# Attention loop of a hybrid decoder layer: all score banks of a job computed in one step instead of two

## The chip, the cores and the metric

The kernel runs on one core of a Trainium2 chip. The metric is the device time of one execution in microseconds (us), as the median of several runs. Less is better.

## What is computed

One post-norm decoder layer over 512 tokens of width 1024, in fp32, with three sublayers: a hybrid mixer, a cross attention over 256 memory rows, and a SwiGLU. The change lies in the mixer, which has three attention branches side by side:

```python
proj = x @ w_in + b_in                        # q, k, v of A, B, C, forget gates, merge gates
# A: 4 heads x 3 dilation groups, banded, T5 bias; groups combined by softmax denominators
# B: 8 query heads over 2 kv heads, window 128, T5 bias, learned sinks
# C: 4 heads, causal, logit bias from cumulated log forget gates
s = einsum(q, k) + bias;  s = where(mask, s, -1e30)
m = max(s);  p = exp(s - m);  o = einsum(p / sum(p), v)
merged = g0*(o_a @ w_a) + g1*(o_b @ w_b) + g2*(o_c @ w_c)
x = layer_norm(ALPHA*x + merged @ w_out)
```

## The kernel before, in words

Every engine has its program written out by hand, and the engines meet only at semaphores. The large matrix products are split into two fp32r parts and run as three matmuls each (`mm3`, L1588); they fill TensorE for most of the time. Between the input projection and the gate stage lies the attention loop, the part that the change touches.

**Jobs.** The attention work is cut into 12 jobs (`make_jobs`, L167). Jobs 0 to 3 are the heads of A, jobs 4 to 7 pairs of heads of B, jobs 8 to 11 heads of C. A job's scores fill up to four PSUM banks; job j's bank b always lies in PSUM bank b (`score_bank`, L511), so banks 0 to 3 are used by one job after the other. Jobs 4 to 8 and job 10 have four banks, jobs 9 and 11 have two. The scores of jobs 0 to 3 are computed ahead of the loop, in the stretch `FRONT`.

**Steps.** The loop has 22 steps (`N_GROUP_PAIRS`), each for a pair of transposition groups. In step i TensorE (L1858 to L1868)
- transposes the probabilities of groups 2i+2 and 2i+3 into PSUM banks 4 and 5 (`turn_probs`, L1741, matmul at L1753). It first waits until the copies of groups 2i and 2i+1 are out of these banks (`pt_act`, `pt_dve`);
- computes scores (`scores`, L1705, matmuls at L1718, for C also L1725), if `SIDE[i]` lists any. `side_work` (L233) lists banks 0 and 1 of a job in one step and banks 2 and 3 in the next: job 4 in steps 1 and 2, job 5 in 3 and 4, job 6 in 5 and 6, job 7 in 7 and 8, job 8 in 10 and 11, job 9 in 12, job 10 in 14 and 15, job 11 in 16;
- in some steps transposes a row of reciprocals (`turn_recip`, L1756, L1762);
- multiplies the transposed probabilities of groups 2i and 2i+1 by V (`times_v`, L1765, matmul at L1789).

VectorE in step i (L1343 to L1356) copies group 2i+3 out of PSUM (`pt_drain`, L1209), now and then inverts the sums of a job (L1193, L1194), drains an output accumulator (`out_drain`, L1229, L1234), and then drains the banks of `SIDE[i]` (`scores_out`, L1157): for each unit of a bank it adds the bias and takes the extreme value (L1181), which is one custom instruction and one that reads the accumulator; the second raises `neg_ready`. ScalarE in step i (L924 to L934) copies group 2i+2 out of PSUM (L865), copies parts of accumulators (L871, L877) and applies the exponential to the banks of the step before, `SIDE[i - 1]` (`exps`, L838, L851).

**What orders a bank's reuse.** `scores` takes the banks of its job two at a time. Ahead of each two it waits on `neg_ready` until VectorE has drained what an earlier job left in these banks:

```python
for some in [banks[i:i + 2] for i in range(0, len(banks), 2)]:
    for b in some:
        prev = [(jj, bb) for jj, bb in bank_list if jj < j and score_bank(jj, bb) == score_bank(j, b)]
        if prev:
            pe.wait_ge(neg_ready, bank_units_end[prev[-1]])
```

`neg_ready` is one counter, raised in VectorE's order of drains.

Names in short, as used below: T is `turn_probs`, V is `times_v`, S01 and S23 are the scores of banks 0 and 1 and of banks 2 and 3, "4;3" is bank 3 of job 4.

Of the kernel before, what the change touches and what calls it, by code (L numbers as in the profile page):

```python
# [44 lines left out]
N_AH, N_G = 4, 3  # L45
# [96 lines left out]
N_SELF = 12  # L142
# [90 lines left out]
def side_work(jobs):  # L233

    side = [[] for _ in range(N_GROUP_PAIRS)]
    for j in range(4, N_SELF):
        first = 2 * j - 7 if j < 8 else C_SCORES_AT[j - 8]
        for b in range(len(jobs[j][0])):  # L240
            side[first + b // 2].append((j, b))
    return side


def build_layer(nc, A, out):
    JOBS = make_jobs() + make_cross_jobs()
    SIDE = side_work(JOBS)
# [62 lines left out]
    with ExitStack() as ctx:  # L310
# [193 lines left out]
        def exps_of(j):  # L504

            return units_before[(j | 1) + 1 if JOBS[j][1][0][2] == "C" else j + 1]

        RECIP_AT = [n + 1 for n in out_begin[N_AH:]]
        SUMS_AT = {j: 2 * j - 4 if j < 8 else C_SCORES_AT[j - 7] + 1 for j in [4, 5, 6, 7, 8, 10]}

        def score_bank(j, b):  # L511
            return b
# [305 lines left out]
        def _(act):  # L818
            def split(p):

                c = chunk_of(p)
                if p == 0:
                    act.wait_ge(first_in, 16)
                else:
                    act.wait_ge(raw_in[c % 2], arrive_at[c])
                if p >= 2:
                    act.wait_ge(piece_done, slot_spent(p))
                src, hi, _ = raw_piece(p)
                act.copy(hi, src).then_inc(hi_done, 1)  # L829
# [43 lines left out]
            def recip_copy(k):  # L873

                act.wait_ge(recip_ps, k - N_AH + 1)
                act.wait_ge(acc_dve, k - 1)
                act.copy(qk[:, T_RECIP + k % 2, :], ps[:, acc_bank(2 * k + 2), :]).then_inc(recip_out, 1)  # L877
# [46 lines left out]
            for i in range(N_GROUP_PAIRS):  # L924
# [4 lines left out]
                if i == 0:  # L929
                    split(PG + 1)  # L930
                if i in RECIP_AT:
                    recip_copy(N_AH + RECIP_AT.index(i))
                for j, b in SIDE[i - 1] if i else []:
# [653 lines left out]
        def _(pe):  # L1587
# [94 lines left out]
            def operands(kind, h, t):  # L1682

                rows = slice(t * P, (t + 1) * P)
                band = slice(max(t - 1, 0) * P, (t + 1) * P)
                half_ = slice(64 * (h % 2), 64 * (h % 2) + 64)
                if kind == "X":
                    return qx[half_, h // 2, rows], kx[half_, h // 2, :]
                if kind == "A0":
                    return qk[half_, T_QA + h // 2, rows], qk[half_, T_KA + h // 2, band]  # L1690
                if kind in ("A1", "A2"):
                    g = int(kind[1])
                    return qk[half_, T_QA + 2 * g + h // 2, rows], qk[half_, T_KA + 2 * g + h // 2, rows]
                if kind == "B":
                    return qk[half_, T_QB + h // 2, rows], qk[half_, T_KB + h // 4, band]
                return qk[half_, T_QC + h // 2, rows], qk[half_, T_KC + h // 2, 0:(t + 1) * P]

            def key_gates(h, n):

                half_ = slice(64 * (h % 2), 64 * (h % 2) + 64)
                return pick[half_, h % 2, h // 2:h // 2 + 1].to_broadcast([64, P]), gates_t[half_, 0:n]

            def scores(j, banks=None):  # L1705

                banks = list(banks or range(len(JOBS[j][0])))
# [5 lines that stand above are left out]
                    n_units = len(JOBS[j][0][some[0]])  # L1713
                    for u in range(n_units):
                        for b in some:
                            kind, h, t, c0, cols, at = JOBS[j][0][b][u]
                            q, k = operands(kind, h, t)
                            ins = pe.matmul(ps[:, score_bank(j, b), c0:c0 + cols], q, k, start=True, stop=kind != "C")  # L1718
                            if u == n_units - 1 and kind != "C":
                                ins.then_inc(score_ps, 1)  # L1720
                        for b in some:
                            kind, h, t, c0, cols, at = JOBS[j][0][b][u]
                            if kind == "C":
                                one, gates = key_gates(h, cols)
                                ins = pe.matmul(ps[:, score_bank(j, b), c0:c0 + cols], one, gates, start=False, stop=True)  # L1725
                                if u == n_units - 1:
                                    ins.then_inc(score_ps, 1)
# [13 lines left out]
            def turn_probs(n):  # L1741

                j, g = group_list[n]
                offs = JOBS[j][1][g][0]
                if N_AH <= j < N_SELF:
                    pe.wait_ge(exp_done, exps_of(j))
                else:
                    pe.wait_ge(prob_pool if j in POOL_SCALES else prob_dve, scaled_for(j, g))
                if n >= 2:
                    pe.wait_ge(*pt_count(n - 2))  # L1750
                kind = JOBS[j][1][g][2]
                for c, at in enumerate(offs):
                    ins = pe.transpose(ps[:, 4 + n % 2, c * P:(c + 1) * P], prob_at(kind, at, P), ident[:, :])  # L1753
                ins.then_inc(pt_ps, 1)

            def turn_recip(k):  # L1756

                pe.wait_ge(recip_wide, k - N_AH + 1)
                pe.wait_ge(acc_dve, k)
                for t in range(TT):  # L1760
                    cols = slice(t * P, (t + 1) * P)
                    ins = pe.transpose(ps[:, acc_bank(2 * k + 2), cols], qk[:, T_WIDE + k % 2, cols], ident[:, :])  # L1762
                ins.then_inc(recip_ps, 1)

            def times_v(n):  # L1765

                work = []
                for i in (n, n + 1):
                    j, g = group_list[i]
                    _, products, kind, h, first, last = JOBS[j][1][g]  # L1770
                    m = acc_of[i]
                    pe.wait_ge(*pt_count(i))
                    if first and m >= FIRST_X + 2:
                        pe.wait_ge(oxl_done, m - 2 - FIRST_X + 1)
                    elif first and 4 <= m < FIRST_X:
                        pe.wait_ge(acc_dve, m // 2 - 1)
                        if m // 2 > N_AH:
                            pe.wait_ge(recip_out, m // 2 - N_AH)
                    src = ptx if j >= N_SELF else pt
                    work.append([(ps[acc_half(kind, h), acc_bank(m), q0:q0 + cols], v_tile(kind, h, kb),  # L1780
                                  src[:, i % PT_SLOTS, c0:c0 + cols], first and x == 0, last and x == len(products) - 1)
                                 for x, (kb, c0, cols, q0) in enumerate(products)])
                a, b = work
                for x in range(max(len(a), len(b))):
                    for one in (a, b):
                        y = x - max(len(a), len(b)) + len(one)
                        if y >= 0:
                            dst, lhs, rhs, start, stop = one[y]
                            ins = pe.matmul(dst, lhs, rhs, start=start, stop=stop, skip_group_check=True)  # L1789
                            if y == len(one) - 1:  # L1790
                                ins.then_inc(av_done, 1)
# [66 lines left out]
            for i in range(N_GROUP_PAIRS):  # L1858
                if i + 1 < N_GROUP_PAIRS:
                    turn_probs(2 * i + 2)  # L1860
                    turn_probs(2 * i + 3)
                if SIDE[i]:
                    scores(SIDE[i][0][0], [b for _, b in SIDE[i]])
                if i in RECIP_AT:
                    turn_recip(N_AH + RECIP_AT.index(i))
                if i == 0:
                    pe.wait_ge(proj_out, 22 + 9)
                times_v(2 * i)  # L1868
# [215 lines left out]
```

## Time and profile before

| what | value |
|---|---|
| median of 3 runs | 907.95 us (907.76, 907.95, 908.62) |
| the profiled execution's own time | 909.56 us |
| its span (first to last instruction) | 907.8 us, granted clock 0.997 |
| attention loop in the trace | 197.6 to 257.75 us |
| steps 1 to 8 (scores of jobs 4 to 7) | 201.15 to 224.84 us |

The times of the rows are in us from the start of the span. In the timeline a row begins with its start and its duration; matmuls overlap, so the length of a phase of TensorE is the distance from its start to the start of the phase behind it. "xN" counts instructions; one fp32 matmul of the program stands as several. In brackets is how long the engine sat idle before the row, and what released it.

### The profile page before, as it was taken

The numbers are of one execution on the slowest core, as the hardware profiler recorded it, in microseconds if no ns is written. First come the engines' busy times: TensorE is split into PE (matmuls) and PEld (weight loads), VectorE is DVE, ScalarE is ACT, GpSimd is POOL, SyncE is SP. The second block draws the span as 40 slices with busy tenths as digits, with TensorE's granted clock in tenths as the row PEclk, the third lists the DMA queues.
The fourth block names the chain that finished last, engine by engine and source line by source line (L and its number), as shares of the span: only waits on it lengthen the run. The fifth ranks groups of instructions, "written<-read, shape, count | busy, mean of one in ns | idle before, by whom it ended". The sixth has DMA issues, their size and how long they took to land.

```text
span 907.8 us, 11620 instructions
## 1 busy us (share of the span) xinstructions
PE 882.0 (97%) x4547; PEld 732.8 (81%) x4547; DVE 424.1 (47%) x795; ACT 290.8 (32%) x536; POOL 59.0 (7%) x87
## 2 busy tenths in 40 slices
PE   7999999999999999999999889999999999999996
PEld 7988887777678888888889679888888888888885
DVE  4244347669632525353766784333333333422344
ACT  3112157129642232222424742222222222111221
POOL 2100000080310000000020020000000000000001
PEclk9999999999999999999999999999999999999999
DMA  7524630321002333326515101233322224222321
GB/s 267 158 93 106 151 94 24 113 80 42 2 1 94 106 105 107 98 92 231 191 42 170 57 6 50 93 103 110 106 94 92 92 92 139 93 93 97 109 96 69
DMA packets 70022, 89.88 MB, mean 99 GB/s; under 512 B 2701, under 2 KB 61911, under 8 KB 69983
## 3 DMA queue, kind: packets, MB, share of 16 engines
q1 hardware_dynamic: 69599, 88.92, 30.3%
q0 software_dynamic: 384, 0.43, 0.3%
q8 instruction: 26, 0.43, 0.2%
q14 instruction: 13, 0.11, 0.0%
HBM read 86.81 MB, written 2.52 MB: 98 GB/s over the span
## 4 chain that ended last, share of the span: by engine, by line
PE 91%; ACT 3%; DVE 3%; issue 1%; DMA 1%; POOL 1%; SPq 0%; DVEq 0%; POOLq 0%; ACTq 0%
PE ps L1590 27%; PE ps L1592 27%; PE ps L1591 27%; PE ps L1789 3%; PE ps L1753 2%; PE ps L1718 2%; ACT prob L851 2%; PE ps L1627 1%; DVE w_lo L1083 1%; PE ps L2061 1%; DMA x_nat<-in_x 1%; PE ps L2062 1%; PE ps L2063 1%; ACT w_hi L829 0%; DVE resid L1423 0%
## 5 line engine op out<-in xcount | busy, mean ns | idle before, releaser
L1590 PE MATMUL ps<-xt_hi,w_hi 128*128 128x512 f32 (+1 forms) x712 | 274.6, 386 | 5.6 <-DVE w_lo L1083 2.7
L1591 PE MATMUL ps<-xt_hi,w_lo 128*128 128x512 f32 (+1 forms) x712 | 273.7, 384 | 0.0
L1592 PE MATMUL ps<-xt_lo,w_hi 128*128 128x512 f32 (+1 forms) x712 | 273.6, 384 | 0.0
L1590 PEld LDWEIGHTS ps<-xt_hi,w_hi 128*128 128x128 f32 x712 | 133.8, 188 | 33.8 <-DVE w_lo L1083 3.5
L1591 PEld LDWEIGHTS ps<-xt_hi,w_lo 128*128 128x128 f32 x712 | 133.8, 188 | 26.5
L1592 PEld LDWEIGHTS ps<-xt_lo,w_hi 128*128 128x128 f32 x712 | 133.8, 188 | 26.4
L829 ACT CAST w_hi<-raw 128x1024 fp32r<-128x1024 f32 (+1 forms) x59 | 60.8, 1035 | 184.5 <-PE ps L1592 172.7
L1083 DVE TENSOR_TENSOR w_lo<-raw,w_hi 128x1024 fp32r<-128x1024 f32 (+1 forms) x59 | 71.4, 1213 | 97.6 <-ACT w_hi L829 97.3
L1546 DVE TENSOR_TENSOR w_lo<-raw,w_hi 128x1024 fp32r<-128x1024 f32 x40 | 48.9, 1222 | 79.1 <-ACT w_hi L1042 79.1
L1367 DVE TENSOR_TENSOR w_lo<-raw,w_hi 128x1024 fp32r<-128x1024 f32 x30 | 36.7, 1224 | 91.5 <-ACT w_hi L968 91.5
L1042 ACT CAST w_hi<-raw 128x1024 fp32r<-128x1024 f32 x40 | 41.9, 1047 | 78.8 <-PE ps L1592 78.8
L1590 PE MATMUL ps<-w_hi,h_hi 128*128 128x512 f32 x144 | 56.0, 389 | 0.0
L1591 PE MATMUL ps<-w_hi,h_lo 128*128 128x512 f32 x144 | 56.0, 389 | 0.0
L1592 PE MATMUL ps<-w_lo,h_hi 128*128 128x512 f32 x144 | 56.0, 389 | 0.0
L811 POOL TENSOR_SCALAR var<-sq_sum 128x1 f32<-128x1 f32 x12 | 9.2, 767 | 628.9 <-ACT squares L986 628.9
L954 ACT ACTIVATE sg<-ps,bias_t 128x512 f32<-128x512 f32 x24 | 16.6, 690 | 88.2 <-PE ps L1592 88.2
L1565 DVE TENSOR_TENSOR ht<-ps,sa 128x512 f32<-128x512 f32 x22 | 15.2, 691 | 60.7 <-PE ps L1592 60.7
L1054 ACT ACTIVATE sa<-ps 128x512 f32<-128x512 f32 x22 | 13.2, 598 | 89.5 <-PE ps L1592 89.5
L968 ACT CAST w_hi<-raw 128x1024 fp32r<-128x1024 f32 x30 | 31.3, 1043 | 24.5 <-PE ps L1592 24.5
L1590 PEld LDWEIGHTS ps<-w_hi,h_hi 128*128 128x128 f32 x144 | 27.0, 188 | 5.7
L1591 PEld LDWEIGHTS ps<-w_hi,h_lo 128*128 128x128 f32 x144 | 27.0, 188 | 5.6
L1592 PEld LDWEIGHTS ps<-w_lo,h_hi 128*128 128x128 f32 x144 | 27.0, 188 | 5.6
(254 smaller groups left out, 1275.5 us busy)
## 6 DMA issues: line engine op xcount, KB each, us to landing
raw<-in_w_in SPq DMA_DIRECT2D x24, 1024.0 KB, 5.0
raw<-in_w_ffn_in SPq DMA_DIRECT2D x22, 1024.0 KB, 4.9
raw<-in_w_ffn_out SPq DMA_DIRECT2D x11, 1024.0 KB, 4.8
raw<-in_w_mix_out SPq DMA_DIRECT2D x4, 1024.0 KB, 4.9
x_nat<-in_x SPq DMA_DIRECT2D x4, 512.0 KB, 6.6
raw<-in_w_branch_b SPq DMA_DIRECT2D x4, 512.0 KB, 3.9
resid<-in_x SPq DMA_DIRECT2D x1, 2048.0 KB, 9.6
raw<-in_w_xkv SPq DMA_DIRECT2D x2, 1024.0 KB, 5.1
```

The source lines that it names most:

```text
L829: act.copy(hi, src).then_inc(hi_done, 1)
L851: act.activation(v, v, ACT.Exp, bias=nm, scale=-1.0, accum_out=dn).then_inc(exp_done, 1)
L968: act.copy(w_hi[p % 2][:, :].rearrange("p (k c) -> p k c", k=KT), v).then_inc(hi_done, 1)
L1042: act.copy(w_hi[p % 2][:, :].rearrange("p (k c) -> p k c", k=KT), v).then_inc(hi_done, 1)
L1083: dve.tensor_tensor(lo, src, f32(hi), ALU.subtract).then_inc(lo_done, 1)
L1367: dve.tensor_tensor(w_lo[s][:, :].rearrange("p (k c) -> p k c", k=KT), v, f32(w_hi[s][:, :]).rearrange("p (k c) -> p k c", k=KT), ALU.subt ...
L1546: dve.tensor_tensor(w_lo[s][:, :].rearrange("p (k c) -> p k c", k=KT), v, f32(w_hi[s][:, :]).rearrange("p (k c) -> p k c", k=KT), ALU.subt ...
L1590: pe.matmul(dst, a_hi, b_hi, start=start, stop=False)
L1591: pe.matmul(dst, a_lo, b_hi, start=False, stop=False)
L1592: return pe.matmul(dst, a_hi, b_lo, start=False, stop=stop)
L1718: ins = pe.matmul(ps[:, score_bank(j, b), c0:c0 + cols], q, k, start=True, stop=kind != "C")
L1789: ins = pe.matmul(dst, lhs, rhs, start=start, stop=stop, skip_group_check=True)
```

## The change

TensorE issues all score banks of a job in the step in which it issued the first two. In the step after it, it issues none. `SIDE`, which VectorE and ScalarE follow, is unchanged, and so is the code of `scores`, with its waits. Jobs 9 and 11 have two banks and stay as they were.

```diff
@@ -505,6 +505,7 @@
 
             return units_before[(j | 1) + 1 if JOBS[j][1][0][2] == "C" else j + 1]
 
+        SCORES_AT = {next(i for i, now in enumerate(SIDE) if (j, 0) in now): j for j in range(N_AH, N_SELF)}
         RECIP_AT = [n + 1 for n in out_begin[N_AH:]]
@@ -1859,8 +1860,8 @@
                 if i + 1 < N_GROUP_PAIRS:
                     turn_probs(2 * i + 2)
                     turn_probs(2 * i + 3)
-                if SIDE[i]:
-                    scores(SIDE[i][0][0], [b for _, b in SIDE[i]])
+                if i in SCORES_AT:
+                    scores(SCORES_AT[i])
                 if i in RECIP_AT:
                     turn_recip(N_AH + RECIP_AT.index(i))
```

`SCORES_AT` is {1: 4, 3: 5, 5: 6, 7: 7, 10: 8, 12: 9, 14: 10, 16: 11} (step: job).

## Rows read from the trace of the kernel before

**Rows 1.** The page, busy time of the engines over the span

```profile
PE 882.0 (97%) x4547; PEld 732.8 (81%) x4547; DVE 424.1 (47%) x795; ACT 290.8 (32%) x536; POOL 59.0 (7%) x87
```

**Rows 2.** Windows, steps 1 to 8 and the rest of the loop (window, its length, busy us)

```profile
201.15:224.84 23.69, 23.66 (x218) 17.54 (x216) 22.92 (x88) 19.86 (x71) 1.43 (x3) 1.00 0.15 46
224.84:257.75 32.91, 31.83 (x245) 19.55 (x243) 18.95 (x61) 21.15 (x64) 11.62 (x14) 1.00 0.01 1
```

**Rows 3.** Timeline of TensorE: T of step 2, then steps 3 to 6, S23 of job 7

```profile
204.05 0.98 PE L1753 MATMUL ps<-ident,prob 128*128 128x128 f32 x7
...
208.07 0.93 PE L1718 MATMUL ps<-qk 64*128 64x128 f32 x8
208.93 1.09 PE L1789 MATMUL ps<-pt,va 128*64 128x128 f32 x12
209.94 1.20 PE L1753 MATMUL ps<-ident,prob 128*128 128x128 f32 x7
211.08 1.14 PE L1718 MATMUL ps<-qk 64*128 64x256 f32 x8
212.14 1.09 PE L1789 MATMUL ps<-pt,va 128*64 128x128 f32 x12
213.16 1.09 PE L1753 MATMUL ps<-ident,prob 128*128 128x128 f32 x8
...
216.06 0.98 PE L1753 MATMUL ps<-ident,prob 128*128 128x128 f32 x7
216.97 1.14 PE L1718 MATMUL ps<-qk 64*128 64x256 f32 x8
...
222.76 1.13 PE L1718 MATMUL ps<-qk 64*128 64x256 f32 x8
```

**Rows 4.** Timeline of VectorE: ends of drains, and copies of transposed groups

```profile
209.68 0.09 DVE L1181 DVE_READ_ACCUMULATOR2_ANT nmax<- 128x1 f32 x1
209.68 0.69 DVE L1209 COPY pt<-ps 128x512 f32<-128x512 f32 x1
...
211.63 0.69 DVE L1209 COPY pt<-ps 128x512 f32<-128x512 f32 x1
...
215.00 0.08 DVE L1181 DVE_READ_ACCUMULATOR2_ANT nmax<- 128x1 f32 x1
...
222.87 0.56 DVE L1209 COPY pt<-ps 128x384 f32<-128x384 f32 x1 [0.37 <-PE ps L1753]
```

**Rows 5.** Timeline: what TensorE starts behind two waits, and ScalarE's last instruction before one

```profile
210.49 0.42 PEld L1753 LDWEIGHTS ps<-ident,prob 128*128 128x128 f32 x4 [0.24 <-issue]
...
251.32 0.19 ACT L851 ACTIVATION_READ_ACCUMULATOR prob<-prob,nmax 128x1 f32 x1
...
251.57 1.09 PE L1753 MATMUL ps<-ident,prob 128*128 128x128 f32 x8 [1.08 <-ACT prob L851]
```

**Rows 6.** Waits, whole span: TensorE's scores for VectorE's drains (us, times, longest)

```profile
PEld ps L1718 <- DVE nmax L1181: 0.3, 2, 0.2
```

**Rows 7.** Timeline: the last drain of job 7, and the scores of job 8 (step 10)

```profile
226.11 0.08 DVE L1181 DVE_READ_ACCUMULATOR2_ANT nmax<- 128x1 f32 x1
...
227.90 0.49 PE L1718 MATMUL ps<-qk 64*128 64x128 f32 x4
```

**Rows 8.** Timeline of ScalarE: copies in step 2 and in step 17

```profile
204.63 0.48 ACT L865 COPY pt<-ps 128x384 f32<-128x384 f32 x1 [2.20 <-PE ps L1753]
205.01 0.58 ACT L871 COPY qk<-ps 64x512 f32<-64x512 f32 x1
...
249.51 0.59 ACT L877 COPY qk<-ps 128x512 f32<-128x512 f32 x1 [0.28 <-PE ps L1762]
```

**Rows 9.** TensorE's clock (windows; the number before the last two), and a timeline row

```profile
250.00:252.00 2.00, 0.92 (x10) 0.58 (x7) 0.20 (x1) 1.51 (x5) 0.13 (x1) 1.00 0.00 0
...
510.00:520.00 10.00, 7.47 (x46) 4.86 (x48) 5.70 (x18) 7.91 (x22) 0.00 (x0) 0.83 0.07 18
...
511.02 0.63 PE L1753 MATMUL ps<-ident,probx 128*128 128x128 f32 x4 [2.25 <-DVE probx L1198]
```

## The prediction

> **What bounds the kernel now.** I read the page first: TensorE is busy for 882.0 of 907.8 us [rows 1], so whatever stops it inside its stream is paid in full, unless it gets it back at a later wait. Then the attention loop, by windows. In steps 1 to 8 TensorE is busy for 23.66 of 23.69 us, and VectorE for 22.92 [rows 2]: two engines full at once, TensorE setting the time, VectorE with 0.77 us to spare in eight steps. Behind step 8 VectorE is busy for 18.95 of 32.91 us. The list of waits says that scores wait for drains for 0.3 us in the whole span [rows 6]: bank reuse costs next to nothing now. The question is what is left of that when banks 2 and 3 are wanted one step earlier.
>
> **The change, part by part.** No matmul, drain or copy is added or removed, and no DMA moves; SP's queue is not touched, and POOL's transfers and copies are not passed by anything. Six S23 phases (jobs 4, 5, 6, 7, 8, 10) move ahead of one V and two T groups. Queued behind a waiting S23 on TensorE are V of the same step and T of the next, so everything else TensorE does.
>
> *Job 4, step 1.* Banks 2 and 3 were last used ahead of the loop. No wait. V and T come one S23 phase (211.08 to 212.14 is 1.06 us [rows 3], for the same shape) later, and step 2 has no scores, so it ends where it did. VectorE and ScalarE are behind TensorE here. Cost 0.
>
> *Job 5, step 3, the first stall.* S01 runs from 208.07 to 208.93 [rows 3]. S23 then needs 4;3 drained, which VectorE does in its step 2. That drain ends at 209.68 + 0.09 = 209.77 [rows 4]. It can't come earlier: VectorE works without a gap there, in an order that stays. So S23 starts at 209.77 + h, where h is the hand-over from VectorE to TensorE, and TensorE stands still for 0.84 + h. A part comes back: T of step 4 now takes 211.08 - 209.94 = 1.14 us, where the same seven transposes take 216.97 - 216.06 = 0.91 [rows 3], because it waits for VectorE's copy of group 9 (209.68 + 0.69 = 210.37 [rows 4]). Moved behind the stall, it finds the copy done: -0.23. Net 0.61 + h.
>
> *Jobs 6 and 7, the coupled stalls.* With the stall, T of group 11 ends late, and VectorE's step 4 begins with the copy of just that group. VectorE so starts late, drains 5;3 late, and TensorE's next S23 (6;2 and 6;3) waits for that. The circle, from the start of one S23 to the start of the next: S23 1.06 (211.08 to 212.14), V 1.02 (212.14 to 213.16), T 0.91 [rows 3], then 0.11 until the copy starts (222.76 to 222.87 [rows 3, 4], where VectorE was waiting), then VectorE's own step from the copy to the last drain, 211.63 to 215.00 + 0.08 = 3.45 [rows 4], then h. Sum 6.55 + h. TensorE's work for the same two steps is 216.97 - 211.08 = 5.89 [rows 3]. Each stall is therefore 0.66 + h. There are two: job 6 in step 5 and job 7 in step 7.
>
> *The hand-over h.* No row shows VectorE's accumulator read releasing scores after a real wait. The nearest ones: VectorE's copy ends at 210.37, the weight load that wanted it starts at 210.49 [rows 5] and its four transposes end a phase at 211.08, 0.71 later, where four of them take 0.52 (seven take 0.91): about 0.20 with the restart of the pipeline. On the other side ScalarE's accumulator read ends at 251.51 and TensorE starts at 251.57 [rows 5]: 0.06. I take h = 0.15, nearer the first, since the engine is the same, and keep 0.06 to 0.20. Less than 0.06 is excluded, as both waits show that much; more is possible and goes into the upper end.
>
> *Jobs 8 and 10, steps 10 and 14.* 7;3 is drained at 226.11 + 0.08 [rows 7], and behind the stalls it comes some 3.2 us later, 229.5 (TensorE's 2.4, and the step in which VectorE now trails S23). S01 of job 8, with 227.90 + 2.4 = 230.3 for its start [rows 7], begins after it, and S23 later still. For job 10 the banks were drained steps ago, and VectorE has 14 us of spare time here [rows 2]. Their S23 only trade places with the next V and T. Cost 0; if that cover were gone, it would be at most another 0.66 + h for each.
>
> *What becomes late next.* ScalarE copies group 2i+2 and an accumulator half before its exponentials. TensorE's wait for it in step 18 (1.08 us [rows 5]) ends a chain that starts from TensorE's own reciprocals: ScalarE's copy at 249.51 was itself released by TensorE [rows 8]. That chain moves with TensorE, so this wait does not give anything back. Behind the loop come products that wait only on TensorE's own pace and on weights fetched ahead; nothing there has a fixed date. The delay reaches the end.
>
> Sum: (0.61 + h) + 2 x (0.66 + h) = 1.93 + 3h = 2.38 us; 2.1 with h = 0.06, 2.5 with h = 0.20. The rows are from one execution with a span of 907.8 us and an own time of 909.56; the span is 0.15 under the median of the runs, 907.95, the own time 1.6 over it. The terms are differences inside the span, so I add them to the median: 907.95 + 2.38 = 910.3.
>
> **Rivals.**
>
> *The slack gives it back.* If ScalarE's exponentials of job 11 can run before the reciprocals' copy, or VectorE's idle time behind step 8 pulls the later waits forward, up to the 1.08 us that TensorE stands still in step 18 come back: 910.3 - 1.08 = 909.2. For it: it is the only real wait of the loop, and VectorE is over 40% idle there. Against: the releaser named for ScalarE is TensorE, and ScalarE's order is fixed. Chance 0.08.
>
> *Not slower.* It is decided at one place: whether 4;3 is drained when S01 of job 5 ends, 208.93. If S23 of job 4, now in PSUM a step earlier, let VectorE get 0.84 us ahead, no stall starts, the circle never closes, and the 0.23 us wait in step 4 vanishes or stays: 907.7 to 907.95. For it: VectorE's input is there sooner. Against: VectorE is busy for 22.92 of 23.69 us [rows 2] and the input is not what it waits for. Chance 0.03.
>
> *ScalarE closes a second circle.* VectorE's accumulator drain in the even steps waits for a half that ScalarE copies. In step 2 T starts at 204.05 [rows 3], ScalarE begins its group copy at 204.63, and the half is copied at 205.01 + 0.58 [rows 8]: 1.54 from T's start. VectorE will want it at 0.91 + 0.11 + 0.69 (its own copy [rows 4]) = 1.71 or later. The margin may be as small as 0.2 us, and exponentials that now begin late stand in ScalarE's queue ahead of it. Eaten up in two of the steps, it would add about 0.5 each: 911.3. Chance 0.06.
>
> *The clock.* The stalls are gaps in TensorE's stream, and TensorE's clock can fall: between 510 and 520 us the mean granted clock is 0.83, with a gap of 2.25 us of TensorE just ahead [rows 9]. Of its two levels, 1.2 and 2.4 GHz, the lower was granted for a part of that window; a mean of 0.83 over 10 us is a loss of 0.17 x 10 = 1.7 us of full-speed time. One such fall gives 912.0, three give 915.4. Against it, in this loop a gap of 1.08 us [rows 5] left the clock at 1.00 [rows 9], and mine are 0.8 to 1.0 us with some 6 us of full work between. Chance 0.04.
>
> The Trainium skill (TensorE: Matmul & The Clock Gate, section on psum-queue depth-cycling) has a rule against this change: short idle times between groups of matmuls, made by cycling through PSUM banks, can be frequent enough that the clock swings between its levels. By that rule the last rival would be the forecast. The trace so far shows the fall only behind a gap more than twice as long.
>
> **How the numbers follow.** The forecast as worked out has 0.79, the others 0.08, 0.03, 0.06 and 0.04. Its own range is 2.1 to 2.5 on 907.95, so 910.0 to 910.5, and with the 0.3 to 0.6 us by which runs of this kernel differ, 909.6 to 911.0. I widen it down to 909.2, for the slack, and up to 911.3, for ScalarE's circle; what is left out is the clock and the case that isn't slower. Within 0.2% (1.8 us, about what a measurement of this kernel can tell from no change) means 906.1 to 909.8. It holds the slack, the case of no stall and the lower edge of the forecast: 0.15. Faster 0.02. Slower by more than 0.2%: 0.83.
>
> **What would show it.** In the changed profile the waits list should have scores waiting for drains (L1718 for L1181) about three times for 2.6 us in all (0.99 + 0.81 + 0.81), in steps 3, 5 and 7, and none in steps 10 and 14. VectorE should sit idle for about 1.3 us ahead of its copies (L1209) in steps 4, 6 and 8. T of step 4 should have lost its wait. Step 9 should start near 227.2 in place of 224.84, and the gate stage near 260.1 in place of 257.75, with the clock at 1.00. Wrong would be: a first stall that is missing (VectorE ahead), stalls that grow from job to job (ScalarE), a shift at 227 us that is smaller at 258 us (slack), or a clock of 0.5 in the loop.

## The result and the profile after

The changed kernel takes 910.83 us in the median of 22 runs (909.62 to 912.21). The kernel before, run beside it, takes 909.01 us (22 runs, 906.07 to 911.50; the three runs known ahead of the prediction lie in the lower half). The ratio is 1.0018, with a 95% interval from 1.0011 to 1.0026: slower by 1.0 to 2.4 us, clear of no change. The ratio itself stays just short of the 0.2% line, which lies inside the interval.

The program ahead of the loop is the same in both kernels and still doesn't take the same time: the loop starts 1.0 us earlier in the changed kernel's trace. So from here on I compare the length of the loop, from the first transpose of step 1 to the first matmul of the gate stage. Before it is 257.75 - 201.15 = 56.60 us. In the changed kernel these two rows of TensorE's timeline read

```profile
200.15 1.09 PE L1754 MATMUL ps<-ident,prob 128*128 128x128 f32 x8
...
258.98 0.50 PE L1591 MATMUL ps<-xt_hi,w_hi 128*128 128x512 f32 x1
```

which is 58.83 us: the loop got longer by 2.23. (The lines behind the new one stand one number higher than before.) Behind the loop nothing differs: from the gate stage to the end of the span it is 650.05 us before and 650.12 after.

The windows of the same two stretches as in [rows 2], here of the changed kernel (window, its length, busy us of PE, PEld, DVE, ACT and POOL, clock, DMA share, GB/s):

```profile
200.15:226.23 26.08, 23.62 (x217) 17.84 (x216) 21.96 (x87) 18.71 (x67) 1.36 (x3) 1.00 0.14 42
226.23:258.98 32.75, 31.36 (x245) 19.66 (x243) 20.07 (x62) 22.11 (x68) 11.61 (x14) 1.00 0.01 2
```

Steps 1 to 8 took 23.69 us and now take 26.08, with TensorE busy for 23.6 in both: the 2.39 us more are standing still. The rest of the loop lost nothing, it even won 0.16. The clock is 1.00 in both. The waits list of the stretch around the loop names the new wait, where [rows 6] had 0.3 us (for the idle matmul unit and for the idle weight loads the same wait is listed twice):

```profile
PEld ps L1719 <- DVE nmax L1182: 3.6, 3, 1.4
PE ps L1719 <- DVE nmax L1182: 2.5, 3, 1.0
```

And TensorE's timeline, steps 3 to 7, which answers to [rows 3]:

```profile
205.84 1.23 PE L1754 MATMUL ps<-ident,prob 128*128 128x128 f32 x8
207.00 0.93 PE L1719 MATMUL ps<-qk 64*128 64x128 f32 x8
208.90 1.13 PE L1719 MATMUL ps<-qk 64*128 64x256 f32 x8 [0.98 <-DVE nmax L1182]
209.97 1.09 PE L1790 MATMUL ps<-pt,va 128*64 128x128 f32 x12
210.99 0.98 PE L1754 MATMUL ps<-ident,prob 128*128 128x128 f32 x7
211.90 1.09 PE L1790 MATMUL ps<-pt,va 128*64 128x128 f32 x12
212.92 1.09 PE L1754 MATMUL ps<-ident,prob 128*128 128x128 f32 x8
213.94 0.93 PE L1719 MATMUL ps<-qk 64*128 64x128 f32 x8
215.61 1.13 PE L1719 MATMUL ps<-qk 64*128 64x256 f32 x8 [0.74 <-DVE nmax L1182]
...
219.63 1.09 PE L1754 MATMUL ps<-ident,prob 128*128 128x128 f32 x8
...
222.32 1.14 PE L1719 MATMUL ps<-qk 64*128 64x256 f32 x8 [0.74 <-DVE nmax L1182]
...
226.23 1.09 PE L1754 MATMUL ps<-ident,prob 128*128 128x128 f32 x8
```

Each time S01 of jobs 5, 6 and 7 is followed by a gap and only then by S23. VectorE's side of the circle, in the same kernel's timeline (answers to [rows 4]):

```profile
212.01 0.69 DVE L1210 COPY pt<-ps 128x512 f32<-128x512 f32 x1 [1.30 <-PE ps L1754]
...
215.38 0.08 DVE L1182 DVE_READ_ACCUMULATOR2_ANT nmax<- 128x1 f32 x1
```

VectorE sits idle for 1.30 us until T of step 4 is done, copies, and has drained 5;3 at 215.46. TensorE's S23 starts at 215.61. The two engines now wait for each other in turn. Before, TensorE had one short wait in steps 1 to 8 (0.23 us in step 4) and VectorE one of 0.37 us (ahead of its copy at 222.87, [rows 4]).

### The profile page after: what moved, and what is told of

The parts are those of the page before. It is cut to its first block, busy times and chain, and to the rows that moved or that the text cites. A ratio compares the mean times of both kernels' runs of the same rounds, so it can differ in the third digit from the quotient of the medians.

```text
span 909.1 us, 11620 instructions
## 1 busy us (share of the span) xinstructions
PE 880.7 (97%) x4547; PEld 732.4 (81%) x4547; DVE 424.0 (47%) x795; ACT 290.5 (32%) x536; POOL 58.9 (6%) x87
## 4 chain that ended last, share of the span: by engine, by line
PE 89%; DVE 5%; ACT 3%; issue 1%; DMA 1%; POOL 1%; SPq 0%; DVEq 0%; POOLq 0%; ACTq 0%
PE ps L1591 27%; PE ps L1593 26%; PE ps L1592 26%; PE ps L1790 2%; ACT prob L852 2%; PE ps L1754 2%; PE ps L1719 1%; PE ps L1628 1%; DVE w_lo L1084 1%; DVE prob L1182 1%; DMA x_nat<-in_x 1%; PE ps L2062 1%; PE ps L2063 1%; PE ps L2064 1%; ACT w_hi L830 1%
```

## The experiments

All runs are judged by two things: the ratio to the kernel before, run beside it, where there is one (its interval is 1.4 to 2.6 us wide), and the length of the loop in the trace. There is one trace of each kernel; that its lengths tell 0.1 us is seen where different kernels share a stretch, as in the first stall, which is 0.98 us in the traces of the changed kernel, of e8_split7 and of e9_dose_after. They are summed up here; what was expected of each, and what follows, stands below.

| kernel | jobs in one go | else | loop, us | against before | ratio (95%) |
|---|---|---|---|---|---|
| before | none | | 56.60 | | |
| changed | 4 to 8, 10 | | 58.83 | +2.23 | 1.0018 (1.0011 to 1.0026) |
| e1_split567 | 4, 8, 10 | | 55.89 | -0.71 | 0.9986 (0.9976 to 0.9997) |
| e2_only567 | 5, 6, 7 | | 59.53 | +2.93 | 1.0030 (1.0016 to 1.0045) |
| e3_only5 | 5 | | 57.39 | +0.79 | one run |
| e8_split7 | 4, 5, 6, 8, 10 | | 57.55 | +0.95 | one run |
| e6_v_between | 4 to 8, 10 | V between S01 and S23 | 56.64 | +0.04 | 1.0002 (0.9989 to 1.0015) |
| e4_drain_first | 4 to 8, 10 | VectorE drains scores first | 55.95 | -0.65 | 0.9981 (0.9970 to 0.9991) |
| e5_before_drain_first | none | VectorE drains scores first | 56.58 | -0.02 | 0.9993 (0.9979 to 1.0006) |
| e7_best | 4, 5, 6, 8, 10 | VectorE drains scores first | 55.77 | -0.83 | 0.9985 (0.9973 to 0.9997) |
| e9_dose_after | 4 to 8, 10 | two memsets on VectorE | 59.94 | +3.34 | one run |
| e10_dose_before | none | two memsets on VectorE | 56.61 | +0.01 | one run |

### Which jobs cost, which gain: e1_split567, e2_only567, e3_only5

The edit in all three, with the set of jobs that are issued as before:

```diff
-                if i in SCORES_AT:
+                if SIDE[i] and SIDE[i][0][0] in (5, 6, 7):
+                    scores(SIDE[i][0][0], [b for _, b in SIDE[i]])
+                elif i in SCORES_AT:
                     scores(SCORES_AT[i])
```

The set is (5, 6, 7) in the first, (4, 8, 10) in the second, (4, 6, 7, 8, 10) in the third.

> Jobs 4, 8 and 10 in one go, jobs 5, 6 and 7 split again as before. Length of the loop, from the first transpose of step 1 to the first matmul of the gate stage: 56.60 us before, 58.83 changed. Theory (the cost is TensorE waiting for VectorE's drains in steps 3, 5 and 7, closed to a circle by the transposes queued behind): no wait of scores for drains, no wait in step 10; what is left is that scores of four banks in a row are shorter by 0.2 us for B and 0.35 for C; job 4's share is eaten by VectorE's copies, so 55.7 to 56.1, some 0.7 us faster than before. Rival (issuing S23 ahead of V costs by itself, whatever is drained): a third to a half of the 2.2 us stays, 57.3 to 57.8. Rival (ScalarE falls behind because its inputs come in lumps): a wait in steps 10 or 11 stays, 56.5 or more.

Measured: 55.89 us, and no wait of TensorE for a drain (the one left in the waits list is the 0.2 us of weight loads known from [rows 6]). With jobs 5, 6 and 7 out, the change is a gain. That S23 comes ahead of V does not cost by itself.

> The other half: only jobs 5, 6 and 7 in one go, jobs 4, 8 and 10 split as before. Loop 56.60 us before, 58.83 changed. Theory: all three waits stay (0.98, 0.74, 0.74 and a little more, as job 4 gives no head start), so does the wait in step 10 of 0.55 us, and the 0.7 us saved at jobs 8 and 10 are missing: 59.3 to 59.7 us, the slowest of all. Rival (the waits depend on how the whole loop is laid out, job 4's scores in one go above all, which makes the transposes of step 2 late): less than 58.8.

Measured: 59.53 us. The waits are the same three, the first a bit shorter than expected:

```profile
209.63 1.13 PE L1719 MATMUL ps<-qk 64*128 64x256 f32 x8 [0.91 <-DVE nmax L1182]
...
216.34 1.13 PE L1719 MATMUL ps<-qk 64*128 64x256 f32 x8 [0.74 <-DVE nmax L1182]
...
223.05 1.13 PE L1719 MATMUL ps<-qk 64*128 64x256 f32 x8 [0.75 <-DVE nmax L1182]
```

The two halves add up: +2.93 and -0.71 make +2.22, and the whole change is +2.23. Steps 1 to 8 take 226.95 - 200.88 = 26.07 us here, 2.38 more than before, and the wait in step 10 (below) adds 0.55. So the change is two changes, a loss at jobs 5 to 7 and a gain at the others, that do not touch each other.

> Only job 5 in one go. Theory (first stall from the distance of the drain, the later ones from the circle that S23 of the next job closes): one wait of 0.98 us in step 3, minus the 0.23 of step 4, and nothing in steps 5 to 8, because VectorE, late by 1.2 us in step 4, has till step 6 for S23 of job 6: loop 57.2 to 57.5 us. Rival (VectorE, once late, stays late and makes TensorE wait for its copies): waits for copies in steps 6 to 8, 57.8 us or more.

Measured: 57.39 us. One wait, in step 3, and none for a drain behind it:

```profile
209.21 1.13 PE L1719 MATMUL ps<-qk 64*128 64x256 f32 x8 [0.91 <-DVE nmax L1182]
...
217.08 1.13 PE L1719 MATMUL ps<-qk 64*128 64x256 f32 x8
```

The transposes of step 6 take 0.96 instead of 0.91 us (216.12 to 217.08), which is all that VectorE's lateness costs in these steps. The later stalls of the changed kernel are not the echo of the first; each needs its own S23 one step early.

### Is it a circle? e9_dose_after and e10_dose_before

One instruction more on VectorE in steps 4 and 6, ahead of the score drains, in the changed kernel and in the kernel before (`spare` names the buffer `pad_line`, which the kernel reserves and never uses):

```diff
-        sb("pad_line", [P, PAD_LINE])
+        spare = sb("pad_line", [P, PAD_LINE])
...
+                if i in (4, 6):
+                    dve.memset(spare[:, :], 0.0)
                 for jj, b in SIDE[i]:
                     scores_out(jj, [b])
```

> The changed kernel with one more instruction of VectorE in steps 4 and 6, a memset of 488 columns, ahead of the score drains; its length d is read from the trace (0.3 to 0.6 us expected, from copies of 512 columns at 0.6 and half as much for a memset). Theory (the circle S23, V, T, copy, drains sets the time of steps 3 to 8): the stalls in steps 5 and 7 grow by d each, from 0.74 to 0.74 + d, the first not at all, and the loop grows by 2d. Rival (TensorE waits because the banks are asked for too early by a fixed amount, not in a circle): VectorE has 1.3 us of idle time per two steps in which d disappears; loop 58.8 to 59.0.

> The same two memsets in the kernel before. Theory: there scores are separated from the drains by a step, no circle is closed, and what d costs is only what VectorE's copies come late for the transposes: 0 to 0.3 us in the loop (56.6 to 56.9), where the changed kernel pays 2d. Rival (VectorE is the bound of steps 1 to 8 as much as TensorE, 22.92 of 23.69 us busy): 2d less 0.77 us or more in both.

VectorE's timeline of the changed kernel with the memset, step 4:

```profile
212.10 0.69 DVE L1230 TENSOR_TENSOR qk<-ps,qk 64x512 f32<-64x512 f32 x1
212.95 0.47 DVE L1357 MEMSET pad_line<- 128x488 f32 x1 [0.17 <-issue]
213.43 0.48 DVE L1182 CUSTOM_DVE_ANT_0 prob<-ps,tab,neg_sink 128x256 f32<-128x256 f32 x1
```

From the accumulator drain to the first score drain it is 1.33 us, where it is 0.72 without the memset (213.04 to 213.76 in the changed kernel): d = 0.61. In step 6 it is 1.22, d = 0.50. (The memset itself takes 0.47 us, more than the half of a copy's 0.6 that had been expected at the low end.) TensorE's waits are now

```profile
207.97 1.14 PE L1721 MATMUL ps<-qk 64*128 64x256 f32 x8 [0.98 <-DVE nmax L1182]
...
215.29 1.13 PE L1721 MATMUL ps<-qk 64*128 64x256 f32 x8 [1.35 <-DVE nmax L1182]
...
222.49 1.14 PE L1721 MATMUL ps<-qk 64*128 64x256 f32 x8 [1.24 <-DVE nmax L1182]
```

The first is untouched. The second grew from 0.74 by 0.61, the third by 0.50, and the loop by 59.94 - 58.83 = 1.11, the sum of both. VectorE is idle for 1.3 us just ahead of each of these steps, and none of that takes up the dose. In the kernel before, the same two instructions cost 56.61 - 56.60 = 0.01 us, though VectorE has less idle time there than in the changed kernel: 0.77 us in steps 1 to 8, less than the dose of 1.11. VectorE falls behind, its idle time ahead of the copies in steps 8 and 10 shrinks (from 0.37 us to nothing and from 1.22 to 0.73), and no scores wait for it in the meantime. So it is not VectorE's load that costs, but that its step lies in a closed chain with TensorE's.

### Two ways to open the circle: e6_v_between and e4_drain_first

```diff
                 if i in SCORES_AT:
-                    scores(SCORES_AT[i])
+                    scores(SCORES_AT[i], [0, 1])
...
                 times_v(2 * i)
+                if i in SCORES_AT and len(JOBS[SCORES_AT[i]][0]) > 2:
+                    scores(SCORES_AT[i], [2, 3])
```

> As the changed kernel, but S23 stands behind V of the same step and not ahead of it (order T, S01, V, S23, in steps 1, 3, 5, 7, 10 and 14). Against the kernel before, S23 is then earlier by one T only. Theory (the stall is the distance between the drain and S23, 0.84 us too little in step 3): V covers it, 1.02 us; no stall in step 3, hardly any in steps 5 and 7 (circle 5.7 us against 5.9 of work). The 0.23 us wait in step 4 goes. Loop 56.1 to 56.6 us, at or a little below before. Rival (VectorE is simply late once anything moves): 0.3 us or more of stall in each of steps 5 and 7, loop 57 or more.

Measured: 56.64 us, just above the range given, for a reason outside of it (a wait in step 10, below). In steps 3, 5 and 7 TensorE does not stand still: from S01 of job 5 to S23 of job 6 the phases touch.

```profile
207.90 0.93 PE L1719 MATMUL ps<-qk 64*128 64x128 f32 x8
208.76 1.09 PE L1790 MATMUL ps<-pt,va 128*64 128x128 f32 x12
209.78 1.13 PE L1719 MATMUL ps<-qk 64*128 64x256 f32 x8
210.84 0.98 PE L1754 MATMUL ps<-ident,prob 128*128 128x128 f32 x7
```

Steps 1 to 8 take 224.45 - 200.98 = 23.47 us, 0.22 less than before, the old wait in step 4. One phase of 1.02 us between S01 and S23 is the whole difference to the changed kernel's 26.08. In step 3 it only just suffices: 4;3 is drained at 209.59 and S23 starts at 209.78, 0.19 us later, where the hand-over alone takes 0.14 to 0.15.

The second way leaves TensorE as changed and turns round VectorE's order in three steps:

```diff
+                drain_first = i in (2, 4, 6)
+                if drain_first:
+                    for jj, b in SIDE[i]:
+                        scores_out(jj, [b])
                 for j in range(N_AH, N_SELF):
                     if SUMS_AT.get(j) == i:
                         sums_out(j)
                 if i - 1 in out_end:
                     out_drain(out_end.index(i - 1))
-                for jj, b in SIDE[i]:
-                    scores_out(jj, [b])
+                if not drain_first:
+                    for jj, b in SIDE[i]:
+                        scores_out(jj, [b])
```

> All jobs in one go as in the changed kernel; VectorE in steps 2, 4 and 6 drains the score banks ahead of its sums and its output accumulator, where it did so behind them. Same instructions. Theory (the circle S23, V, T, copy, drain sets the pace of steps 3 to 8): it gets 0.72 us shorter in step 2 and 1.1 in steps 4 and 6, to about 5.6 us against 5.7 of TensorE's own work, so the waits of 0.98 and 0.74 us shrink to 0.2 in step 3 and to nothing in steps 5 and 7; loop 54.9 to 55.6 us, 1.0 to 1.7 us faster than before the change. Rival (VectorE has too little spare time at all, whatever its order): the waits stay at 0.5 us or more each and the loop at 58 or more. Rival (ScalarE is next): waits for ScalarE's copies take the place of the gain, loop 56 to 57.

Measured: 55.95 us. The stalls went as expected: S01 and S23 of job 5 take 2.12 us together (1.72 without a wait, so 0.40 is left, twice what I gave; the other 0.20 is what joining the two phases saves, which brings S23 to the wait sooner), those of jobs 6 and 7 take 1.72.

```profile
206.56 2.19 PE L1724 MATMUL ps<-qk 64*128 64x128 f32 x16
208.68 1.09 PE L1795 MATMUL ps<-pt,va 128*64 128x128 f32 x12
...
212.66 1.79 PE L1724 MATMUL ps<-qk 64*128 64x128 f32 x16
214.38 1.09 PE L1795 MATMUL ps<-pt,va 128*64 128x128 f32 x12
```

But the loop missed its range, and the same 0.55 us wait in step 10 is the reason: without it, it would be 55.40. (T of step 10 waits there for ScalarE's copy and then for VectorE's, 0.16 us of idle time named for each, so the second rival has a part in it, though the loop stays below its 56.)

> The kernel before with only VectorE's new order in steps 2, 4 and 6 (score banks ahead of sums and output accumulator). Control for the run with both. Theory (the order matters only where scores wait for drains): loop 56.4 to 56.8 us, no difference that can be measured. Rival (the new order is a gain of its own): 56.1 or less.

Measured: 56.58 us, and the interval of the ratio holds 1. The new order is worth nothing by itself.

### The wait in step 10: e8_split7 and e7_best

In the changed kernel, V and T of steps 9 and 10 read

```profile
227.69 0.87 PE L1790 MATMUL ps<-pt,vbc 128*64 128x256 f32 x8
228.73 1.19 PE L1754 MATMUL ps<-ident,prob 128*128 128x128 f32 x6 [0.17 <-ACT pt L866]
229.84 0.49 PE L1719 MATMUL ps<-qk 64*128 64x128 f32 x4
```

From V's start to the scores it is 2.15 us; before it was 1.60 (226.30 to 227.90). T waits for copies that ScalarE and VectorE make only behind the drains and exponentials of step 8, the later of them VectorE's copy of group 21. It reads, first before, then in the changed kernel

```profile
226.11 0.69 DVE L1209 COPY pt<-ps 128x512 f32<-128x512 f32 x1
```

```profile
228.56 0.68 DVE L1210 COPY pt<-ps 128x512 f32<-128x512 f32 x1
```

T of step 8 starts at 221.95 and 224.41. So the copy begins 4.16 us behind it before and 4.15 us in the changed kernel: VectorE is not late. TensorE is early, by the S23 phase of 1.06 us that no longer stands in step 8.

> As the changed kernel, job 7 alone split again; VectorE's order untouched. Theory A for the wait in step 10: steps 8 and 9 without scores bring TensorE back too soon. Then it vanishes (0.55 us) with the third stall (0.8): loop 58.83 - 1.35 = 57.4 to 57.6 us, though the first two stalls and their lateness of VectorE and ScalarE stay. Theory B (lateness that builds up over jobs 5 to 7): the wait in step 10 stays at 0.3 us or more, loop 57.8 to 58.1.

Measured: 57.55 us; from V to the scores it is 226.19 - 224.55 = 1.64. The wait is gone although the first two stalls, 0.98 and 0.74 us, are there and VectorE's copy of group 21 begins 4.76 us behind T of step 8 (224.91 - 220.15), later than in either kernel of the case. So the wait comes from the two steps in a row without scores, not from lateness that builds up.

> Candidate: jobs 4, 5, 6, 8 and 10 in one go, job 7 split, VectorE draining the score banks first in steps 2, 4 and 6. Theory for the wait in step 10 (0.55 us in all kernels with job 7 in one go or with its S23 in step 7): steps 8 and 9 then both hold no scores, TensorE gets back to the transposes of step 10 before VectorE's long step 8 and ScalarE's exponentials are over. With job 7's S23 in step 8 it should vanish, at the price of 0.2 us for the joined phase: loop 55.4 to 55.8 us, 0.9 to 1.2 faster than before. Rival (the wait comes from ScalarE's lateness that builds up over jobs 4 to 6): it stays, 56.0 or more.

Measured: 55.77 us, at the upper end; V to scores takes 225.49 - 223.75 = 1.74, so 0.14 of the wait is left. This kernel, e4 and e1 are all faster than the kernel before, by 0.14 to 0.19% as measured, and so than the changed one; their intervals overlap, and no order among them is shown. The simplest is e1, the change without jobs 5, 6 and 7.

## Why the prediction was right, and where not

**The bound and the mechanism** held. TensorE's stream sets the end, and the 2.23 us by which the loop grew reached the end of the span in full (650.05 and 650.12 us behind the loop).

**Job 5, first stall.** Predicted 0.84 + h with h = 0.15, so 0.99. The row says 0.98, but that is counted from the end of the last matmul of S01; counted as in the prediction, from 207.00 + 0.86 = 207.86 to 208.90, it is 1.04. The 0.23 us of step 4's T came back. At the start of step 5 the changed kernel is 212.92 - 200.15 = 12.77 us into the loop, before it was 12.01: +0.76, as predicted (0.61 + h). The match is a little too good: the stall is 0.05 longer, since S01 came 0.07 earlier against the drain, and the 0.06 gained at job 4 (below) hides it.

**Jobs 6 and 7, the circle.** Predicted 0.81 each. At step 7 it is 219.63 - 200.15 = 19.48 against 17.91: +1.57, so 0.81. At step 9 it is 26.08 against 23.69: +2.39, so 0.82, against the sum of 2.38.

**The hand-over.** 5;3 is drained at 215.46, S23 begins at 215.61: 0.15, the value taken from between 0.06 and 0.20. In the other two stalls it is 0.14.

**Job 4** was put at 0 and is about that, but from two parts that I had not seen: S01 and S23 without a phase between them take 1.72 us (201.17 to 202.89 in the changed kernel) instead of 0.86 + 1.06, and 0.14 of the 0.20 is lost again as T of step 3 waits for VectorE's copy (1.16 instead of 1.02).

**Jobs 8 and 10** were put at 0. This step failed in detail. TensorE gained 0.35 and 0.36 us there, and lost 0.55 in step 10, a wait that I had not seen since I looked only at the banks and not at what an emptied step 8 brings forward. The three nearly cancel (-0.16), so the sum was right with a part of luck: 2.38 predicted, 2.23 in the trace. The prediction named a shift that is smaller at the end of the loop than at step 9 as a sign of slack; the shift did shrink, from 2.39 to 2.23, but from these terms, not from slack.

**The rivals.** *Slack gives it back*: the wait in step 18 is 1.08 us as before, nothing came back. *Not slower*: 4;3 was drained 0.9 us after S01 ended; VectorE got no head start from having its input sooner. *ScalarE's second circle*: its copies were in time in steps 2 to 8, and stall three is no longer than stall two. The margin was as thin as feared in step 8: ScalarE's half is copied at 226.08, VectorE's drain starts at 226.22. *The clock*: with three gaps of up to 0.98 us, and in the dose experiment of up to 1.35, the granted clock of the loop is 1.00. The Trainium skill (TensorE: Matmul & The Clock Gate, section on psum-queue depth-cycling) tells of a kernel in which short idle times between groups of matmuls came often enough to make the clock swing. That did not happen here, where some six us of work lie between two gaps.

**The numbers.** 910.83 lies in the range 909.2 to 911.3. The move, 1.82 us between medians, is smaller than the 2.38 forecast; its interval, 1.0 to 2.4 us, holds the 2.23 of the traces and just about reaches 2.38. The base was 1.1 us too low, since three runs had stood for the kernel before, and the 0.3 to 0.6 us by which runs were taken to differ are too little: the 22 runs lie 5.4 us apart. The two errors have opposite signs. From the base of 909.01 the same sum gives 911.39, just outside the range, so that 910.83 lies inside is in part luck as well. The chance of 0.83 for "slower by over 0.2%" was too sure: the forecast of 0.26% lay only 0.06% beyond the line, and the measured 0.18% is short of it. With differences of this size the side of the line is decided by terms like the ones I set to 0.

## What to carry to other kernels

Before moving work ahead in one engine's order, ask of each wait in it how long ago its releaser finished, and what stands between: here a 1.02 us phase of V was the cover for a drain that ended 0.84 us too late. If the releasing engine's step itself starts from something queued behind the moved work, the wait is no one-off but a circle that is paid each round. On VectorE's part of it each us added cost one us (1.11 for 1.11), whatever its busy share says; TensorE's part was not lengthened in any run. And don't take a change of this kind whole: by groups of jobs, it was +2.93 and -0.71.

## What the hardware showed that I had not expected

Phases of TensorE that differ in their operands cost at each boundary. Its weight loads idle for 0.17 us at most boundaries, but for 0.33 where V follows scores, as in this stretch of the changed kernel's weight loads:

```profile
201.16 1.39 PEld L1719 LDWEIGHTS ps<-qk 64*128 64x128 f32 x16 [0.17 <-issue]
202.88 0.85 PEld L1790 LDWEIGHTS ps<-pt,va 128*64 128x64 f32 x12 [0.33 <-issue]
203.90 0.75 PEld L1754 LDWEIGHTS ps<-ident,prob 128*128 128x128 f32 x7 [0.17 <-issue]
204.82 0.85 PEld L1790 LDWEIGHTS ps<-pt,va 128*64 128x64 f32 x12 [0.17 <-issue]
```

Joining S01 and S23 takes a boundary away, worth 0.20 us for B and for C alike (for job 8 the scores take 1.34 + 0.74 us before and 231.72 - 229.84 = 1.88 joined). For C there are 0.15 us more: in the step after it T is now followed directly by the transposes of the reciprocals (L1763), and the two take 0.93 + 0.53 us where with scores between them they took 1.02 + 0.59. In e6_v_between, which keeps S01 and S23 apart, the 0.20 are missing and the 0.15 are there. That it is the change of operands that costs is argued from these rows; no run varied the operands alone.

The start of the kernel varies more than the whole effect. In the ten traces of the variants the loop begins between 197.8 and 201.3 us, with the same code ahead of it. Part of it is when TensorE's matmuls reach full pace. Two rows at nearly the same time, the first of the kernel before, the second of the changed one, in the timelines of TensorE:

```profile
12.07 0.41 PE L2061 MATMUL ps<-w_hi,xt_hi 128*128 128x256 f32 x1
```

```profile
12.08 0.28 PE L2063 MATMUL ps<-w_hi,xt_lo 128*128 128x256 f32 x1
```

A matmul of 256 columns takes 0.41 us in one and 0.28 in the other; the slow pace lasts until 13.8 us in the first and until 11.9 in the second, and the matmuls follow each other at 0.21 us in it and at 0.12 behind it. The block of matmuls starts at 11.29 us in one and at 11.21 in the other, and the transposes behind it at 13.99 and 13.03: 0.88 of the 1.0 us between the starts of their loops arise here. The clock column of the profile reads 1.00 in both stretches, so it is the durations that tell it. Another part is when the first inputs arrive: TensorE waits for them for 6.0 us in the trace of before and for 4.9 in that of e8_split7. Neither has to do with the change, and both are in every time measured.
